# Squares of the gated scan rows on ScalarE, a low part behind the second scanned row, and gates by tanh

## What is computed

```python
y = (y_f + jnp.flip(y_b, 1) + xs * d_skip[:, None]).reshape(b, l, SSM_INNER)   # branch 1: the scan
y = rms_norm(y * jax.nn.silu(z), norm_g)
...
gates = jax.nn.sigmoid(proj[..., OFF_GATE:N_IN].reshape(b, l, N_BRANCHES, D_MODEL))
merged = (gates[:, :, 0] * (y_att @ w_branch[0])
          + gates[:, :, 1] * (y_ssm @ w_branch[1])
          + gates[:, :, 2] * (y_gm @ w_branch[2]))
return merged @ w_o, k, v, h_fin
```

## Time and profile before

| | us |
|---|---|
| median of 3 runs | 1294.22 |
| lowest and highest run | 1288.75, 1295.73 |
| the profiled execution | 1292.93 |
| its span (first to last instruction) | 1291.1 |
| PE, DVE, ACT busy in it | 1215.4, 970.8, 740.6 |
| mean granted TensorE clock | 0.966 |

### The profile page before, as it was taken

The page is one execution under the profiler, slowest core; times in us unless marked ns, Lnnn a source line. Parts: engine busy times, 40 slices in busy tenths (PEclk is TensorE's granted clock), DMA queues, the critical chain, the costliest instruction groups (busy, mean ns, idle before and its releaser), DMA issues.

```text
span 1291.1 us, 15762 instructions
## 1 busy us (share of the span) xinstructions
PE 1215.4 (94%) x5950; PEld 950.3 (74%) x5953; DVE 970.8 (75%) x1159; ACT 740.6 (57%) x700; POOL 74.5 (6%) x121
## 2 busy tenths in 40 slices
PE   5999999999999999999979999998998999999994
PEld 1667777777677788887857777877777778788883
DVE  1645657787589889888878375768968988988887
ACT  1543553753467677677753255546437776777773
POOL 0401000101000000000020000010000000000000
PEclk8899998989999999999999999988999999999997
DMA  9978864636879999999976777445347999999991
GB/s 355 301 269 305 301 209 140 192 112 260 331 272 355 378 361 340 354 353 348 364 213 234 274 256 273 164 138 184 135 164 256 362 373 352 353 345 364 349 357 65
DMA packets 99491, 358.83 MB, mean 278 GB/s; under 512 B 9188, under 2 KB 12736, under 8 KB 83024
## 3 DMA queue, kind: packets, MB, share of 16 engines
q1 hardware_dynamic: 87504, 295.12, 63.2%
q0 software_dynamic: 11904, 62.63, 14.1%
HBM read 352.92 MB, written 5.83 MB: 278 GB/s over the span
## 4 chain that ended last, share of the span: by engine, by line
PE 65%; DVE 15%; DMA 8%; ACT 6%; issue 3%; DVEq 2%; ACTq 1%; SPq 1%; POOL 0%; POOLq 0%
PE bank L940 61%; DVE wl L1816 7%; DMA raw<-in_moe_w 5%; PE bank L943 4%; ACT wh L1721 2%; ACT wh L1511 2%; DMA first<-in_w_ada 1%; DMA adaw<-in_w_ada 1%; DVE tmp L1816 1%; DMA decay<-decay_rows 1%; DVE seg L2291 1%; ACTq L1606 0%; DVE xbc L2085 0%; DVE xbc L2082 0%; DVE x L1816 0%
## 5 line engine op out<-in xcount | busy, mean ns | idle before, releaser
L1816 DVE TENSOR_TENSOR wl<-raw,wh 128x2048 fp32r<-128x2048 f32 (+1 forms) x268 | 607.6, 2275 | 126.7 <-ACT wh L1511 67.0
L1721 ACT ACTIVATE wh<-raw 128x2048 fp32r<-128x2048 f32 x192 | 367.7, 1916 | 63.8 <-PE bank L940 28.4
L940 PE MATMUL bank<-wh,xgh 128*128 128x512 f32 x512 | 210.1, 410 | 0.0
L940 PE MATMUL bank<-wh,xgl 128*128 128x512 f32 x512 | 203.6, 398 | 0.0
L1511 ACT ACTIVATE wh<-raw 128x2048 fp32r<-128x2048 f32 (+1 forms) x76 | 142.3, 1872 | 100.2 <-PE bank L940 57.5
L940 PE MATMUL bank<-wh,hTh 128*128 128x512 f32 x448 | 186.2, 416 | 4.4 <-DVE wl L1816 2.5
L940 PE MATMUL bank<-wl,hTh 128*128 128x512 f32 x448 | 182.4, 407 | 0.0
L940 PE MATMUL bank<-wh,hTl 128*128 128x512 f32 x448 | 181.8, 406 | 0.0
L940 PE MATMUL bank<-wl,xgh 128*128 128x512 f32 x512 | 140.3, 395 | 0.0
L940 PEld LDWEIGHTS bank<-wl,xgh 128*128 128x128 f32 x512 | 96.1, 188 | 23.5 <-DVE wl L1816 0.2
L940 PEld LDWEIGHTS bank<-wh,xgl 128*128 128x128 f32 x512 | 97.1, 190 | 20.2
(11 more groups left out here) (303 smaller groups left out, 1480.1 us busy)
## 6 DMA issues: line engine op xcount, KB each, us to landing
raw<-in_moe_w SPq DMA_DIRECT2D x256, 512.0 KB, 5.2
raw<-in_moe_w SPq DMA_DIRECT2D x64, 1024.0 KB, 7.2
raw<-in_w_in SPq DMA_DIRECT2D x52, 1024.0 KB, 5.6
adaw<-in_w_ada POOLq DMA_DIRECT2D x32, 1024.0 KB, 5.7
raw<-in_w_branch SPq DMA_DIRECT2D x12, 1024.0 KB, 5.3
raw<-in_w_ada SPq DMA_DIRECT2D x8, 1024.0 KB, 9.9
raw<-in_w_o SPq DMA_DIRECT2D x8, 1024.0 KB, 4.9
first<-in_w_ada SPq DMA_DIRECT2D x4, 1024.0 KB, 16.7
```

Source lines behind the costliest of these rows:

```text
L940: return behind(nc.tensor.matmul(*args, **kw))
L1721: tally(A_(wh[c][:, :], raw[:, r, :], ACT.Copy), part_high[c])
L1816: return V.tensor_tensor(o, a, b, op)
```

## The change

Three things change, in each of the two layers.

1. The gates are no longer a sigmoid. ACT computes tanh(x / 2) (the scale 0.5 is an immediate of the instruction), and DVE, which multiplied the gate by the branch's bank with one `tensor_tensor`, now computes (gate + 1) * bank with one `scalar_tensor_tensor`. So `merged` is twice what it was, and the factor 0.5 is taken back where `merged` is turned: as the scale of ACT's four copies `hTh`, and as the scalar of DVE's four low parts `hTl`, which become `scalar_tensor_tensor` too.
2. The square and the sum over the row leave `scanned(s)` on DVE. ACT does both in one `Square` with `accum_out`: once before the last pair of gates, once behind `branch_turned(2)`. Two semaphores are new: `z_scanned` from DVE to ACT, `z_squared` back.
3. The low part that DVE made in step n = 7 (of the piece ("branch", 2, 1)) is made behind `scanned(1)`.

```diff
@@ ACT: gate_take, the end of the scan, the turned rows
-                        frees(A_(dst[:, s, n * 512:(n + 1) * 512], t[:, :], ACT.Sigmoid), name)
+                        frees(A_(dst[:, s, n * 512:(n + 1) * 512], t[:, :], ACT.Tanh, scale=0.5), name)
...
+                def squared(s):
+
+                    act.wait_ge(z_scanned, 2 * l + s + 1)
+                    A_(tmp[:, NW:D], z[:, s, :], ACT.Square, accum_out=small[:, s:s + 1])
+                    act.drain().then_inc(z_squared, 1)
+
+                squared(0)
                 gate_take(1, 1)
                 branch_turned(2)
+                squared(1)
                 ahead(("branch", 2, 0))
                 square_root(1)
...
-                           ACT.Copy).then_inc(turned_high, 1)
+                           ACT.Copy, scale=0.5).then_inc(turned_high, 1)
@@ DVE: turned, merge, scanned, the end of the scan
+                    if scale is None:
+                        frees(tt(low, t, high.bitcast(F32), ALU.subtract), name)
+                    else:
+                        frees(V.scalar_tensor_tensor(out=low, in0=t, scalar=scale, in1=high.bitcast(F32), op0=ALU.mult, op1=ALU.subtract), name)
...
+                    def gated(out, t, s, hs):
+                        return V.scalar_tensor_tensor(out=out, in0=gates_[:, s, hs], scalar=1.0, in1=t[:, :], op0=ALU.add, op1=ALU.mult)
...
-                            frees(tt(out, t[:, :], gates_[:, s, hs], ALU.mult), f"br{b}{h}{s}")
+                            frees(gated(out, t, s, hs), f"br{b}{h}{s}")
...
-                    tt(z[:, s, :], y, z[:, s, :], ALU.mult)
-                    drain()
-                    tt(tmp[:, NW:D], z[:, s, :], z[:, s, :], ALU.mult)
-                    drain()
-                    V.tensor_reduce(small[:, s:s + 1], tmp[:, NW:D], X, ALU.add)
-                    drain()
+                    tt(z[:, s, :], y, z[:, s, :], ALU.mult).then_inc(z_scanned, 1)
...
-                    if 1 <= n < 8:
+                    if 1 <= n < 7:
                         ahead(SCAN_FILL[n - 1])
                     if n == 6:
                         scanned(0)
                 branch_turned(2)
                 scanned(1)
+                ahead(SCAN_FILL[6])
+                dve.wait_ge(z_squared, 2 * l + 2)
                 V.tensor_scalar(small[:, 2:4], small[:, 0:2], 1.0 / NW, None, ALU.mult)
```

More of the change, by code:

```diff
@@ L550, in hybrid_backbone @@
         y_sem = sem("y_sem")
+        z_scanned = sem("z_scanned")
+        z_squared = sem("z_squared")
         var_ready = sem("var_ready")
@@ L1919, in low, with turned @@
                     tt(hTl[part], merged[:, s, first * P:end * P].rearrange("p (c t) -> p c t", t=P), hTh[part].bitcast(F32), ALU.subtract).then_inc(hT_ready, 1)
-                def turned(b, name, high, low):
-                    t = bank[USE[l][name][0]]
+                def turned(b, name, high, low, scale=None):
+                    t = bank[USE[l][name][0]][:, :].rearrange("p (c t) -> p c t", c=4)
                     dve.wait_ge(turned_high, l * 10 + b + 1)
-                    frees(tt(low, t[:, :].rearrange("p (c t) -> p c t", c=4), high.bitcast(F32), ALU.subtract), name)
+                    if scale is None:
+                        frees(tt(low, t, high.bitcast(F32), ALU.subtract), name)
+                    else:
+                        frees(V.scalar_tensor_tensor(out=low, in0=t, scalar=scale, in1=high.bitcast(F32), op0=ALU.mult, op1=ALU.subtract), name)
                 def branch_turned(b):
@@ L2152, in merge @@
                                 t = bank_full(dve, l, f"br{b}{h}{s}")
-                                frees(tt(tmp[:, s * 512:(s + 1) * 512], t[:, :], gates_[:, s, hs], ALU.mult), f"br{b}{h}{s}")
+                                frees(gated(tmp[:, s * 512:(s + 1) * 512], t, s, hs), f"br{b}{h}{s}")
                                 drain()
@@ L2338, in _ @@
                         part = (slice(None), slice(4 * h, 4 * h + 4), slice(s * P, (s + 1) * P))
-                        turned(6 + 2 * s + h, f"mT{s}{h}", hTh[part], hTl[part])
+                        turned(6 + 2 * s + h, f"mT{s}{h}", hTh[part], hTl[part], 0.5)
                 ahead(("wo", 3))
```

## The result

The changed kernel takes 1282.74 us, the median of 13 runs (1276.54 to 1288.62); the kernel before, run beside it, 1293.09 (13 runs, 1288.75 to 1298.76). The two medians differ by 10.35 us. The ratio is 0.9925, with a 95% interval of 0.9904 to 0.9946, which is 9.7 us faster, between 7.0 and 12.4. A gain of 5.1 was forecast and nearly twice that was measured; 1.1 of the 6.3 comes from a lower median of the kernel before (1293.09 here, 1294.22 when the forecast was made). That the time still fell inside the range is luck as much as working. The profiled execution took 1279.13 us, its span is 1277.3 and its mean granted clock 0.976; before they were 1292.93, 1291.1 and 0.966.

What follows compares the result with a forecast made beforehand. PE, busy 94% of the span, was taken as the bound. -9.9 (z, both layers) + 4.8 (clock) = -5.1 from 1292.93 gives 1287.8; the median's 1.3 more makes 1289.1, rounded to 1289.0 us; range 1282.5 to 1293.5.

Steps and rivals of the forecast that it cites:

- part 1: Scan, layer 0: without the table loads W of step 4 comes 3.4 us earlier, step 4 gains 2.5, low clock's 1.6 goes.
- part 2: Scan, layer 0: square, sum and low part off DVE's path; step 7 comes 6.8 us earlier, product z 6.1.
- part 3: ACT behind product z: the chain to z's turning takes 6.2 us instead of 4.0, a price of 2.2 per layer.
- To z: Turning of z: 6.0 us earlier in layer 0 and 3.9 in layer 1, together 9.9.
- part 4: PE before z's turning: idle of 3.2 us per layer, then low clock costing 2.4 per layer (0 to 2.9), together 4.8.
- part 5: Gates on ACT and DVE: tanh as long as the sigmoid, gated product 0.69 us, so nothing; upper end 1.1 per layer.
- Sum: Whole kernel: -9.9 us to z plus 4.8 of clock loss, a gain of 5.1.
- the clock holds: Rival, PE behind the idle before z: no clock loss or a covered one, so -9.9 us, 1284.3; chance 0.20.
- The drain: Root's table load on ACT: a skill's added 1.38 us per layer would make the total -2.3; the prediction rejected it.
- the swallowed gain: Rival, first experts after each mixer: bandwidth-bound weight transfers lose half the gain, -2.5 us, 1291.7; chance 0.12.

Runs made afterwards that it cites:

- the run with the low part unmoved: Changed kernel with ACT's root ahead of the conversion and DVE's low part back in step n = 7; 1282.09 us, ratio 0.9941 to the kernel before.
- root first: Changed kernel with ACT's square root and its table load ahead of the conversion; 1277.17 us, ratio 0.9878 to the kernel before.
- the load early: Changed kernel with ACT's root before the conversion, a one-column root before the second square, DVE's low part before `uTl`; 1277.44 us, ratio 0.9865.

## Why the prediction was right, and what it mis-sized

- **Loads and step 4 (part 1).** Forecast: no wait at step 4 in layer 0, step 5 6.5 behind step 4. Measured: no wait, 6.50 (255.39 to 261.89). Right, with slack: the exponential came 3.56 behind the conversion for 3.34 (ACT stood idle 0.45 before it), and `seg` of step 5 3.0 earlier, counted from step 0, for 3.4. In layer 1 a wait of 0.51 stayed at step 4.
- **Square, sum and low part (part 2).** Product z 6.1 earlier; measured 5.96 in layer 0 (42.85 behind step 0 instead of 48.81) and 6.81 in layer 1 (43.99, 50.80). Right in layer 0. In layer 1, 0.7 short: I carried layer 0's number over, but there the idle at step 4 had been 3.06 with twelve low matmuls behind. The two causes were told apart rightly: with tanh and the low part moved, but square and sum left on DVE, step 7 doesn't wait and step 6 waits 1.14 and 1.85. It was the later expectation of the run with the low part unmoved that gave square and sum a share in step 7's wait.
- **ACT's order behind product z (part 3).** 6.2 per layer; measured 6.09 in both (layer 1: 894.63 to 900.72). The square with the sum took 0.63 and 0.19 (0.82) between its bounds of 0.57 and 1.33, and the conversion began 0.88 behind the square's start for 0.85. Right. The root stands 0.02 behind its load (277.58 + 1.28 = 278.86, 278.88). With the drain of 1.38 us that the Trainium skill states (ScalarE: Activation LUTs, What ACT_TABLE_LOAD costs) z would, as an estimate, have come at 282.2; it came at 280.8. The trace disagrees with that rule here too.
- **To z.** 6.0 + 3.9 = 9.9 forecast, 5.93 + 4.73 = 10.7 measured in the profiled pair, 9.7 as the mean of the two executions of each kernel.
- **The clock behind the new idle (part 4).** The idle came as forecast (2.90 and 2.89 for 3.2), the loss didn't: 2.4 per layer forecast, 1.35 and 1.53 measured, and none in layer 1 of the second execution. This is the mis-sized term: 4.8 for both layers, measured 2.9 in the profiled pair and 2.1 in the mean. I took the middle of two spells that followed shorter idles, and treated as a price what is a draw: over these traces an idle of 2 to 3 us was followed by anything from no to twelve low matmuls. The second of the two spells was also reckoned 0.2 too long: the same stretch of work takes 6.8 us at the full clock, not 6.6 (layer 1: 7.30 less an idle of 0.53).
- **Arithmetic of the gates (part 5).** 0.69 and 0.59: nothing, right.
- **Sum.** 7.8 in the two scans for 5.1. The timed 9.7 is 1.9 more, but its interval reaches down to 7.0. Outside the scans the profiled executions show no gain (1143.0 and 1142.7 above); with executions this far apart one of 2 or 3 us would not be seen, so that much stays open.
- **The parts.** That tanh alone does in time what the whole change does (0.9923, 0.9925) the prediction didn't say. Squares and moved part together add 1.5 us in the scans' mean (139.87 to 138.4), and nothing clear of noise in time.

Of the rivals, "the clock holds" (1284.3) is nearest to the median. Its reason, a clock that holds, didn't happen in the profiled execution, and happened in one of four scans' ends of the changed kernel. The drain and the swallowed gain are excluded: the former by the 0.02 us above, the latter by a total whose whole interval (7.0 and more) lies above half of what the marks gained.

Where did the 7.8 come from? Idle gave 2.7. The clock gave most of the rest: before, the three spells behind steps 4, 7 and 4 cost 8.12 - 6.50 = 1.6, 9.54 - 6.8 = 2.8 and 9.70 - 6.58 = 3.1 us (888.80 to 898.50 before, 874.85 to 881.43 after); after, two cost 1.35 and 1.53. That is 4.6 less, and 2.7 + 4.6 = 7.3; the other 0.5 are not traced. The third spell is the longest; its two ends in the kernel before and the same two steps of the changed one:

```profile
898.50 0.33 PE L940 MATMUL bank<-xs,W 128*128 128x64 f32 x2
```

```profile
881.43 0.33 PE L942 MATMUL bank<-xs,W 128*128 128x64 f32 x2
```

Before, step 5 of layer 1 came 9.70 behind step 4 at 888.80; after, 6.58 behind 874.85. The waits for W were dear mainly through what the clock did behind them.

## What to carry to other kernels

When an engine's work is moved to another, write down the whole queue of the receiver behind the new wait. Here a square of 0.82 us put a conversion of 1.9 and a table load of 1.3 on the path, and one line exchanged takes z 1.6 us nearer to its product. And price a wait on PE as idle plus what the clock does behind it: a wait of 2 to 3 us can cost the same again, so removing one can pay double and shifting it elsewhere can pay nothing.

## What the runs showed of the chip

- In 57 runs of the unchanged kernel, 1282.29 to 1302.52 us, time and mean granted clock go together (correlation -0.87, 10 us per 0.01 of clock, 0.959 to 0.974). So the spread of a kernel that is the same each time goes largely with its time at 1.2 GHz; which execution gets how much of it, no run here explains. The changed kernel's median clock is 0.972 to the 0.966 of before.
- Twelve unused bf16 matmuls in PE's gap of 2.9 us (eleven stand in the row shown) were followed by the full clock in both layers of one execution, where the gap itself was followed by low spells of 1.35 and 1.53 us, and in a second execution of the changed kernel by one of 1.4 and by none. Gaps of 1.30 and 1.32 were followed by no low matmul (root first), one of 1.46 by seven and another of 1.46 by none (the load early, its two layers).
- Tanh, Square and the exponential stand next to each other without a load, and a `Square` with `accum_out` of 512 columns is 0.61 to 0.63 us plus 0.19.
- `scalar_tensor_tensor` of 128 x 512 out of a bank with an immediate takes 0.68 us, like `tensor_tensor`.
